# All filler matmuls on the identity taken out of a two-layer trunk kernel

## What is computed

```python
h = rms_norm(x, norm_mix[0])
x = x + pool_mixer(h, pool_w, pool_b, pool_scale)        # windows 2, 4, 8, 16
x = x + swiglu(rms_norm(x, norm_ffn[0]), w1, w3, w2)     # dense, 3584 wide
k, v = shared_kv(rms_norm(x, norm_kv), w_kv, b_kv, pos)
h = rms_norm(x, norm_mix[1])
x = x + swa_sink_attention(h, k, v, mask, w_q, b_q, sinks, w_o, b_o, pos)
x = x + moe_swiglu(rms_norm(x, norm_ffn[1]), router_w, w1, w3, w2)  # top 2 of 8
return rms_norm(x, norm_final)
```

## Time and profile before

| | us |
|---|---|
| three runs | 1395.91, 1402.08, 1401.9 (median 1401.9) |
| the profiled execution, its own time | 1398.2 |
| its span, first to last instruction | 1396.4 |
| mean granted clock of TensorE in it | 0.985 |

### The profile page before, as it was taken

The page is one execution under the profiler, slowest core; times in us unless marked ns, Lnnn a source line. Parts: engine busy times, 40 slices in busy tenths (PEclk is TensorE's granted clock), DMA queues, the critical chain, the costliest instruction groups (busy, mean ns, idle before and its releaser), DMA issues.

```text
span 1396.4 us, 18005 instructions
## 1 busy us (share of the span) xinstructions
PE 1368.4 (98%) x6637; PEld 1142.4 (82%) x6637; DVE 1091.9 (78%) x805; ACT 899.8 (64%) x756; POOL 26.3 (2%) x18
## 2 busy tenths in 40 slices
PE   8999999988999999999999999999999999999997
PEld 7888888886888888888888888888888888888885
DVE  5454545596389889888888988888898889888886
ACT  5444334544367777777777777777777777776774
POOL 2000000130000000000000000000000000000000
PEclk9999999986999999999999999999999999999999
DMA  9955555431459999998999999899999999998950
GB/s 348 391 183 189 198 186 181 153 121 46 136 183 372 376 336 348 373 376 316 367 374 338 346 375 375 317 365 376 341 342 373 377 338 345 377 370 315 375 211 32
DMA packets 177718, 413.28 MB, mean 296 GB/s; under 512 B 7641, under 2 KB 13826, under 8 KB 177682
## 3 DMA queue, kind: packets, MB, share of 16 engines
q1 hardware_dynamic: 175696, 410.58, 81.3%
q10 hardware_dynamic: 1666, 1.10, 0.3%
q0 software_dynamic: 320, 1.11, 0.2%
HBM read 411.73 MB, written 1.05 MB: 296 GB/s over the span
## 4 chain that ended last, share of the span: by engine, by line
PE 94%; DVE 3%; ACT 1%; issue 1%; DMA 0%; ACTq 0%; DVEq 0%
PE bank L468 28%; PE bank L470 28%; PE bank L469 28%; PE bank L574 2%; PE bank L476 2%; PE bank L655 1%; PE bank L502 1%; PE bank L501 1%; DVE low L1005 1%; DVE rope_z L1181 1%; PE bank L513 1%; PE bank L512 1%; ACT high L792 0%; PE bank L665 0%; PE bank L677 0%
## 5 line engine op out<-in xcount | busy, mean ns | idle before, releaser
L1005 DVE TENSOR_TENSOR low<-raw,high 128x2048 fp32r<-128x2048 f32 x387 | 882.0, 2291 | 212.7 <-ACT high L792 211.2
L792 ACT ACTIVATE high<-raw 128x2048 fp32r<-128x2048 f32 x387 | 740.1, 1917 | 209.8 <-PE bank L470 209.1
L468 PE MATMUL bank<-high,xg_hi 128*128 128x512 f32 x896 | 351.4, 392 | 0.7 <-DVE low L1005 0.7
L470 PE MATMUL bank<-low,xg_hi 128*128 128x512 f32 x896 | 348.9, 389 | 0.0
L469 PE MATMUL bank<-high,xg_lo 128*128 128x512 f32 x896 | 348.7, 389 | 0.0
L468 PEld LDWEIGHTS bank<-high,xg_hi 128*128 128x128 f32 x896 | 168.2, 188 | 37.8 <-DVE low L1005 3.5
L470 PEld LDWEIGHTS bank<-low,xg_hi 128*128 128x128 f32 x896 | 168.2, 188 | 35.4
L469 PEld LDWEIGHTS bank<-high,xg_lo 128*128 128x128 f32 x896 | 168.3, 188 | 34.2
L468 PE MATMUL bank<-high,hm_hi 128*128 128x512 f32 x448 | 180.6, 403 | 0.0
L470 PE MATMUL bank<-low,hm_hi 128*128 128x512 f32 x448 | 175.4, 391 | 0.0
L469 PE MATMUL bank<-high,hm_lo 128*128 128x512 f32 x448 | 174.7, 390 | 0.0
(11 more groups left out here) (161 smaller groups left out, 1101.8 us busy)
## 6 DMA issues: line engine op xcount, KB each, us to landing
raw<-in_moe_w SPq DMA_DIRECT2D x336, 1024.0 KB, 5.1
raw<-in_ffn_w SPq DMA_DIRECT2D x42, 1024.0 KB, 5.3
raw<-in_w_q SPq DMA_DIRECT2D x4, 1024.0 KB, 5.0
raw<-in_w_o SPq DMA_DIRECT2D x4, 1024.0 KB, 4.9
x_res<-in_x SPq DMA_DIRECT2D x2, 512.0 KB, 4.9
raw<-in_pool_w SPq DMA_DIRECT2D x1, 1024.0 KB, 10.1
raw<-in_w_kv SPq DMA_DIRECT2D x1, 1024.0 KB, 5.7
out_x<-xn SPq DMA_DIRECT2D x2, 512.0 KB, 3.0
```

The source lines that it names most:

```text
L468: pe.matmul(o, s_hi, m_hi, start=start, stop=False)
L470: return pe.matmul(o, s_hi, m_lo, start=False, stop=stop)
L792: act.activation(high[hslot(u)][:], raw[r][:], ACT.Copy).then_inc(split_hi, 1)
L1005: dve.tensor_tensor(low[slot(u)][:], raw[slot(u)][:], high[hslot(u)][:].bitcast(F32), ALU.subtract).then_inc(split_lo, 1)
```

## The change

Both helpers and all their calls go out of PE's program; nothing else is changed. The waits around them, the semaphores and the DMAs stay as they are.

```diff
-            def keep_warm(bank, n):
-                for _ in range(n):
-                    pe.matmul(banks[bank][:, 0:P], ident, ident, start=True, stop=True)
-
-            def keep_warm_narrow(bank, n, rounds):
-                for i in range(rounds):
-                    for g in range(4):
-                        pe.matmul(banks[bank][32 * g:32 * g + 32, 0:n], ident[:, 32 * g:32 * g + 32],
-                                  consts[:, g % 2 * P:g % 2 * P + n], start=True, stop=True)
...
             pe.wait_ge(consts_in, 16)
-            keep_warm(0, 12)
             pe.wait_ge(xn_ready, NT)
...
-            keep_warm(0, 20)
             turn_stream(x_res, x_ready, 0, bank=2)
             feed_forward(PASSES[0], 0)
-            keep_warm_narrow(0, 256, 3)
-            keep_warm_narrow(1, 128, 4)
-            keep_warm(0, 16)
             turn_stream(xn, xn_ready, NT, bank=0)
...
-            keep_warm(0, 5)
...
-            keep_warm(7, 26)
             turn_stream(xn, gained, 0, bank=4)
-            keep_warm(2, 2)
             pe.wait_ge(misc_in, 16 * 2)
...
             mm.then_inc(routed, 1)
-            keep_warm(7, 6)
             pe.wait_ge(chosen_ready, 1)
...
             def expert_pass(ps):
-                if not ps.p0:
-                    keep_warm(7, 5)
                 pe.wait_ge(picked, ps.lists + 1)
                 pe.wait_ge(xs_lo_ready, NT)
                 if ps.p0:
                     pe.wait_ge(added, 2 * ps.p0)
                 gather()
-                if not ps.p0:
-                    keep_warm(0, 9)
...
-            keep_warm(0, 14)
             pe.wait_ge(last_lo, 1)
             scatter(last_scattered)
```

## The result

| | before | without fillers |
|---|---|---|
| median (lowest to highest), us | 1401.26 (1394.38 to 1403.6) | 1406.27 (1401.07 to 1408.01) |
| runs | 13 | 13 |
| span of the profiled execution | 1396.4 | 1401.6 |

The ratio of the changed kernel to the one before is 1.0040, 95% interval 1.0024 to 1.0056: about 5.6 us slower, inside the 7 us that I had called no change, and within the range. The forecast was +4.4 us; the two spans differ by 5.2.

The account below looks back on a forecast made before the run. TensorE bounds the kernel (94% of the chain), so fillers matter only at waits between stages: 1.5 + 2.2 - 2.0 - 0.5 + 3.2 + 0 = +4.4 us on a mean of 1399.5 gives 1403.9, range 1397 to 1412.

Parts of the forecast that it names:

- The start: Twelve fillers before the band matmuls: these start 0.7 us earlier but lose 2.2 at half clock; +1.5, ends +0.9 and +2.7.
- T: Length of half clock once dense work is back: taken as 4.6 us, ends 3.4 and 5.7; loses 0.47 of it.
- rival C: Slower: half clock lasts 10 us after each wait, stages being broken by small waits; +15.4 us, 1414.9; chance 0.13.
- The dense layer: Twenty fillers before it: no earlier start, since PE waits for a_lo, but half clock costs +2.2 us, ends 0 and +2.7.
- Behind the dense layer: 28 narrow and 16 wide fillers: b_hi 2.3 us earlier, passing through to the scores; -2.0, ends -2.4 and -1.0.
- the slack: First query block, ready 2.0 us before DVE comes to it: covers PE's 2.0 us half-clock loss in K, V and queries.
- Scores to projection: After attention: output projection starts earlier without the fillers there; -0.5 us, ends -0.6 and +1.0.
- the five fillers: Fillers after attention, holding the output projection from 346.36 to 347.00; removal forecast at -0.5 us.
- rival B: Clock survives the shrunken wait before the scores; scores save 0.9 us, last query block 2.5; total +1.0, 1400.5; chance 0.18.
- Router to expert: Output projection to first expert: slower router +0.7, gather at half clock +1.7, first expert +0.8; +3.2 us, ends -2.4 and +6.4.
- rival A: Router's 8-column matmuls do not slow at half clock, so the gather starts earlier; total +1.3 us, 1400.8; chance 0.12.
- The end: Fourteen fillers before the last scatter: it starts 1.2 us earlier, given back at half clock; 0, ends -1.2 and +0.4.

Follow-up runs that it names:

- the five groups: Only the fillers between output projection and first expert (26, 2, 6, 5, 9) taken out of the kernel before: median 1401.6 us, ratio 1.0009.
- the other of the two traces: Profiled execution of the kernel before with only the fillers ahead of the last scatter cut from 14 to 8: median 1400.28 us, ratio 0.9994.
- fitted: Kernel before with fillers resized to each wait, 8 wide ones kept after the dense layer, four between the projection's two tiles: median 1392.40 us, ratio 0.9948.

## Why the prediction was right, and where it was not

*The method held.* The time was 2.4 us above the forecast and in the range, on the slower side but within 0.5%, as forecast. No wait appeared but those that the prediction had named, and the expert loop kept its pace: from the first expert's matmul to the last the two kernels differ by 0.84 us, with half clock at its beginning until 402.0 (3.9 us).

*The start: right mechanism, mis-sized by 2.5 us.* The first band matmul came 0.70 earlier, as read. The half clock behind it lasted about 10.1 us and not 4.6, so the term was +4.0 (up to 5.8 in the kernel with the dense fillers alone) against +1.5, outside my ends of +0.9 and +2.7. The failing step is "how long is T once dense work is back": I took the length from the fillers' and the 256-column matmuls' recoveries and carried it to a stream of another kind. With the 16-column matmuls widened and nothing else, T was 4.3 and the term +1.4. This is rival C for the start alone, with its number (+4.0), but not with its reason (small waits): the widened stream had the same two short pauses and recovered in 4.3 us. C's conditions elsewhere did not hold.

*The dense layer: right.* +2.5 against +2.2, for 5.3 us of half clock against 4.6; the first matmul waited for a_lo, the transposes did not keep the clock, and 512 columns at half clock took 0.43 us.

*Behind the dense layer: right in size; the hidden loss shows only elsewhere.* -2.1 against -2.0. But in this trace there was no loss on PE for the slack to hide: the clock was down for 3.4 us while PE waited and transposed (0.59 from 275 to 279), and back when K's first matmul started at 279.13, whose followers come 0.11 us apart. That the slack covers such a loss is shown by the kernel without the fillers behind the dense layer, with 4 us of half clock in K and V and the same 2.1 us gained.

*Scores to projection: a gain for the most part unforecast.* -0.6 is the five fillers (the projection's shift goes from +3.31 at the end of the query block to +2.75). The other -1.1 is a part of rival B: in the changed kernel the clock fell during the scores (0.94 in 309 to 310) and not before them, 2.78 us for 16 in place of 3.80. But the wait before the scores had not shrunk, as B supposed: it was 3.44 us, since PE had lost nothing in K and V. In the five other kernels without the fillers behind the dense layer it was 1.7 to 2.0 us, and in four of them the gain from the scores' start to the end of the last query block was 2.6 us: B's mechanism, worth 2.6 of the 3.4 us that it was priced at. Where the wait was 3.4, that gain was nothing in three traces and 1.1 to 1.3 in five, so the wait alone does not decide it.

*Router to expert: the parts moved about, the sum nearly right.* h_t came 1.2 earlier (1.4 forecast). The router ran at full clock but for its end in this execution (3.93 us), so it did not hold back the counting, as in rival A, but not for A's reason: with the clock low the same 32 instructions take 6.83 us, my 6.8. Of the six kernels without fillers there four took 6.83 us and two 3.9. The counting cost 0.9 (1.0 forecast). So the gather started 1.3 earlier against the projection's end and not 0.7 later, while it ran wholly at half clock, +2.8 against +1.7; its stream did not raise the clock in the 7 us that it lasted. These two errors of opposite sign leave +2.4 against +3.2. A load of 128 weight columns takes 0.21 us at half clock and 0.11 at full, with 8 moving columns as with 128. The Trainium skill (TensorE: Matmul & The Clock Gate, section LDWEIGHTS) gives columns over 1.2 GHz and no second figure, which makes an estimate of 0.107 us at either level; the traces agree with it at full clock and contradict it at half. By it the router would not have slowed; rival A as the page would have it is refuted.

*The end: right*, 1.2 earlier at the scatter's start (shift +3.97 after +5.17) and all given back by its half clock.

*What the median hides.* The base was a mixture. By their times and granted clocks, most executions of the kernel before probably ran the gather at half clock already, so most of what I booked as a loss there (+2.8, +0.8) exists only against the profiled execution. That fits what taking the five groups out costs: 1.3 us by medians and 4.5 by traces. The start's cost is likewise larger in medians (5.3 us) than in the profiled pair, whose execution of the changed kernel (1403.37) is the second lowest of 13; the trace with the dense fillers alone shows that the start can cost 5.8. The two errors nearly cancel in the total; part of its closeness is luck.

Not settled: why some executions of the kernel before have the clock up in the gather (in the profiled one it rose at 388.6, 1.0 us after the gather's start; in the other of the two traces only at 398.9); what makes the group below 1396; and what exactly the 1.83 us hole is. Nor is it settled what it is in a stream that raises the clock: the gather's matmuls have 128 moving columns like the fillers' and the widened band's, and the same pace, and yet the clock stayed down; their operands are rounded halves where the others are plain float32, but no run varies that.

## What to carry to other kernels

A filler is worth what the work behind it loses at half clock if PE leads there, and costs what it outlasts its wait: size each to its own wait from the timeline, fill short gaps between two tiles too, and do not judge them as one set (all out: +5.6 us; twelve kept: none of it; fitted: -7.3). Ask how the stream that follows behaves on its own: a stage such as the band product or the gather here may stay at half clock for nearly its whole length, and then fillers ahead of it that bring the clock up can pay for themselves several times (twelve at the start were worth some 5 us and held the band back by 0.7). When a kernel's times fall in groups, look for a stage whose clock differs between two executions before trusting a comparison with one trace.

## What the hardware showed that I had not expected

- Back-to-back matmuls do not by themselves raise the clock: band products of 128, 16 and 128 columns stayed at half clock for 10.1 us in one trace and for all of their 11 us in another, the gather for its 7 us, the 8-column fillers at the start for all of their stay, while with the 128-column fillers (from 5.5 us to about 9.7) and the widened band (4.3 us) it came up.
- The windows show a granted clock of 1.00 before the first change on record, also where the pace is 0.21 us per load (13 to 19 us in the changed kernel). The pace is the better witness there.
- 1.83 us without any wait between two fillers near the end, in the trace of one layout of the program, and not in that of another.
